# Two transformer blocks on one core: five expert loads put among the second block's weight loads, three raw buffers there, and each expert's six halves loaded in a row

## The reference, cut to what matters

```python
g_prob = softmax(xt @ w_rg + b_rg); g_w, g_idx = top_k(g_prob, 1)
e_top, e_loc = top_k(e_logits_of_that_group, 2)
e_w = softmax(e_top) * g_w
...
def run_block(args):
    xb, e = args
    return (silu(xb @ w_gate[e]) * (xb @ w_up[e])) @ w_down[e]
...
x = x + gate2 * ffn
return rms_norm(x, g_final)
```

## Time and profile before

| | |
|---|---|
| median of 3 runs | 1094.51 us |
| the profiled execution, its own time | 1095.95 us |
| its span, first to last instruction | 1094.2 us |
| mean granted TensorE clock | 0.98 |
| PE busy | 1022.7 us (93%) |
| DVE, ACT busy | 493.4 us (45%), 389.9 us (36%) |
| read from HBM over the span | 325.88 MB, 299 GB/s |

### The profile page before, as it was taken

One profiled execution on the slowest core, in us unless ns is written; L12 is line 12 of the kernel. 1 busy time (PEld: TensorE's weight loads), 2 busy tenths in 40 slices (PEclk: granted clock), 3 DMA queues, 4 the chain that ended last, 5 costly groups with the idle time before them and its releaser, 6 DMA issues.

```text
span 1094.2 us, 13601 instructions
## 1 busy us (share of the span) xinstructions
PE 1022.7 (93%) x5616; PEld 700.9 (64%) x5616; DVE 493.4 (45%) x683; ACT 389.9 (36%) x575; POOL 22.3 (2%) x42
## 2 busy tenths in 40 slices
PE   5999999999999999798999699999999999999883
PEld 4888878888999888697787444444444444443331
DVE  4477667987967745765645511111111111101003
ACT  5644544446435443664734221111111111111112
POOL 0000000010000000100000000000000000000000
PEclk9999999999999999898999799999999999999997
DMA  9977448976887655354444699999999999999991
GB/s 332 338 256 258 160 164 294 315 268 224 287 300 260 235 198 187 104 179 127 181 154 162 265 405 421 421 421 421 422 420 421 421 420 422 421 420 421 422 394 45
DMA packets 86305, 327.87 MB, mean 300 GB/s; under 512 B 5744, under 2 KB 5776, under 8 KB 61536
## 3 DMA queue, kind: packets, MB, share of 16 engines
q1 hardware_dynamic: 84896, 323.45, 77.0%
q0 software_dynamic: 1344, 3.50, 1.0%
HBM read 325.88 MB, written 1.05 MB: 299 GB/s over the span
## 4 chain that ended last, share of the span: by engine, by line
PE 40%; DMA 13%; DVE 3%; ACT 2%; issue 1%; DVEq 0%; ACTq 0%
PE bank L899 15%; DMA e_wlo<-in_w_expert_up 8%; PE bank L922 7%; PE bank L868 3%; DMA es<-in_w_expert_up 3%; DMA raw<-in_w_expert_up 2%; PE bank L937 2%; PE bank L539 2%; PE bank L540 2%; PE bank L543 1%; PE bank L908 1%; PE bank L511 1%; PE bank L515 1%; PE bank L514 1%; PE bank L883 1%
## 5 line engine op out<-in xcount | busy, mean ns | idle before, releaser
L1441 DVE TENSOR_TENSOR wlo<-raw,whi 128x2048 fp32r<-128x2048 f32 x90 | 205.9, 2290 | 105.8 <-ACT whi L985 105.2
L985 ACT ACTIVATE whi<-raw 128x2048 fp32r<-128x2048 f32 x90 | 171.6, 1912 | 98.3 <-PE bank L515 37.9
L2032 DVE SCALAR_TENSOR_TENSOR YL<-bank,wsl,YH 128x512 fp32r<-128x512 f32 x32 | 24.0, 751 | 269.1 <-ACT YH L1369 269.1
L899 PE MATMUL bank<-raw,XT 128*64 128x512 f32 x400 | 90.8, 596 | 5.2 <-DMA raw<-in_w_expert_up 5.2
L899 PE MATMUL bank<-e_whi,XT 128*64 128x512 f32 x192 | 88.5, 604 | 6.7 <-DMA e_wlo<-in_w_expert_up 6.7
L514 PE MATMUL bank<-wlo,hh 128*128 128x512 f32 x224 | 88.5, 395 | 2.9 <-DVE wlo L1441 2.9
L511 PE MATMUL bank<-whi,hh 128*128 128x512 f32 x224 | 89.2, 398 | 1.0 <-ACT whi L985 1.0
L899 PE MATMUL bank<-e_wlo,XT 128*64 128x512 f32 x192 | 88.6, 605 | 0.0
L515 PE MATMUL bank<-whi,hl 128*128 128x512 f32 x224 | 88.3, 394 | 0.0
L539 PE MATMUL bank<-fh,whi 128*128 128x256 f32 x256 | 73.6, 287 | 1.2 <-DVE fl L1611 1.2
L1430 DVE SCALAR_TENSOR_TENSOR ada_acc<-raw,silu_c,ada_acc 128x512 f32<-128x512 f32 x96 | 72.0, 750 | 2.5
(11 more groups left out here) (359 smaller groups left out, 1902.5 us busy)
## 6 DMA issues: line engine op xcount, KB each, us to landing
raw<-in_w_in SPq DMA_DIRECT2D x42, 1024.0 KB, 5.4
raw<-in_w_ff SPq DMA_DIRECT2D x32, 1024.0 KB, 5.4
raw<-in_w_expert_gate SPq DMA_DIRECT2D x25, 1024.0 KB, 22.3
raw<-in_w_expert_up SPq DMA_DIRECT2D x25, 1024.0 KB, 23.0
raw<-in_w_ada SPq DMA_DIRECT2D x24, 1024.0 KB, 5.9
e_whi<-in_w_expert_gate SPq DMA_DIRECT2D x24, 1024.0 KB, 24.2
e_wlo<-in_w_expert_up SPq DMA_DIRECT2D x24, 1024.0 KB, 25.2
raw<-in_w_expert_down SPq DMA_DIRECT2D x22, 1024.0 KB, 25.2
```

Source lines behind the costliest of these rows:

```text
L899: m = e.matmul(b[64 * w:64 * w + 64, :], K.XT[j // 4 % 2][:, k, j % 4, :], K.weights(halves[w])[:, 512 * c:512 * c + 512], start=k == 0, s ...
L985: e.activation(whi[n % RING][:, :], raw[h.raw][:, :], ACT.Copy).then_inc(S["hi"], 1)
L1441: e.tensor_tensor(wlo[n % RING][:, :], raw[h.raw][:, :], whi[n % RING][:, :].bitcast(F32), ALU.subtract).then_inc(S["lo"], 1)
```

## The change

It has four parts. (1) Halves 96 to 113 use only the first three raw buffers (`i % (RAW // 2)` from `LATE` on), and a half waits for the one that was last in its buffer, kept as `before`. (2) The list of the experts' sixteen buffers becomes `es12`, raw3, raw4, raw5, `es7`, raw0, raw1, raw2, then as before; SP issues loads 0 to 4 after halves 98, 99, 100, 101 and 112. (3) The loads' order becomes expert by expert: gate, up, gate, up, down, down, so that expert j's are loads 6j to 6j + 5. (4) PE's order of use stays. `used_up` holds for every expert half its place in that order, and replaces the load's own number where a semaphore's value is wanted.

```diff
+LATE = 96
...
-        self.raw = i % RAW
-        self.loaded = 16 * (i // RAW + 1)
+        self.raw, self.before = raw, before
+        self.loaded = before.loaded + 16 if before else 16
...
+            raw = i % RAW if i < LATE else i % (RAW // 2)
+            half = Half(i, kind, src, chunks, info, len(self.of[kind]), raw, self.in_raw.get(raw))
+            self.in_raw[raw] = half
...
+        self.used_up, n_used = {}, 0
         for base, n, one in ((0, NE, fixed), (NE, NOV, moving)):
+            for j in range(n):
+                for w, hf in ((0, 0), (1, 0), (0, 1), (1, 1), (2, 0), (2, 1)):
+                    one(j, w, hf)
             for j in range(n + 1):
-                for hf in range(2 if j < n else 0):
-                    one(j, 0, hf)
-                    one(j, 1, hf)
+                for w, hf in ((0, 0), (1, 0), (0, 1), (1, 1)) * (j < n):
+                    n_used += 1
+                    self.used_up[base + j, w, hf] = n_used
                 for hf in range(2 if j > 0 else 0):
-                    one(j - 1, 2, hf)
+                    n_used += 1
+                    self.used_up[base + j - 1, 2, hf] = n_used
...
         buffer(slot("es12", 12, [128, 2048]), "es12", 0)
-        buffer(slot("es7", 7, [128, 2048]), "es7", 0, "mix_mm", MIX["m"] + 4)
-        for h in self.halves[-RAW:]:
-            buffer(self.raw[h.raw], f"raw{h.raw}", h.loaded, "lo", h.nth + 1)
+        for r in (*range(RAW // 2, RAW), None, *range(RAW // 2)):
+            if r is None:
+                buffer(slot("es7", 7, [128, 2048]), "es7", 0, "mix_mm", MIX["m"] + 4)
+            else:
+                h = self.in_raw[r]
+                buffer(self.raw[r], f"raw{r}", h.loaded, "lo", h.nth + 1)
...
-        if h.i >= RAW:
-            o = K.halves[h.i - RAW]
+        o = h.before
+        if o:
...
         if i >= n:
-            e.wait_ge(S["eused"], i - n + 1)
+            e.wait_ge(S["eused"], K.used_up[K.experts[i - n][1:]])
...
+    early = {LATE + 2 + k: k for k in range(4)}
+    early[len(K.halves) - 2] = 4
     for h in K.halves:
         load(h)
-    for i in range(K.n_static):
+        if h.i in early:
+            load_expert(early[h.i], K.experts[early[h.i]][0])
+    for i in range(len(early), K.n_static):
```

More of the change, by code:

```diff
@@ L60, with __init__ @@
 class Half:
-    def __init__(self, i, kind, src, chunks, info, nth):
+    def __init__(self, i, kind, src, chunks, info, nth, raw, before):
         self.i, self.kind, self.src, self.chunks, self.info = i, kind, src, chunks, info
         self.nth = nth
-        self.raw = i % RAW
-        self.loaded = 16 * (i // RAW + 1)
+        self.raw, self.before = raw, before
+        self.loaded = before.loaded + 16 if before else 16
 class Sems(dict):
@@ L219, in order_weights @@
         A, self.halves, self.of, n_ada = self.A, [], {"mm": [], "ada": []}, [0]
-        self.half_of = {}
+        self.half_of, self.in_raw = {}, {}
         def add(kind, src, chunks, info=None):
-            self.of[kind].append(Half(len(self.halves), kind, src, chunks, info, len(self.of[kind])))
-            self.halves.append(self.of[kind][-1])
+            i = len(self.halves)
+            raw = i % RAW if i < LATE else i % (RAW // 2)
+            half = Half(i, kind, src, chunks, info, len(self.of[kind]), raw, self.in_raw.get(raw))
+            self.in_raw[raw] = half
+            self.of[kind].append(half)
+            self.halves.append(half)
         def cols(w, r0, c0):
@@ L271, in expert @@
             self.half_of[j, w, hf] = len(self.experts)
-            self.experts.append((src, j))
+            self.experts.append((src, j, w, hf))
         def fixed(e, w, hf):
@@ L1351, in gate_up @@
         def gate_up(j):
-            e.wait_ge(S["eused"], K.half_of[j, 1, 1] + 1)
+            e.wait_ge(S["eused"], K.used_up[j, 1, 1])
             if j > 1:
@@ L1364, in down @@
         def down(j):
-            e.wait_ge(S["eused"], K.half_of[j, 2, 1] + 1)
+            e.wait_ge(S["eused"], K.used_up[j, 2, 1])
             e.wait_ge(S["pt"], 2 * j + 2)
@@ L1375, in gathered @@
             if p > 1 and q == 1:
-                e.wait_ge(S["eused"], K.half_of[4 * p - 5, 1, 1] + 1)
+                e.wait_ge(S["eused"], K.used_up[4 * p - 5, 1, 1])
             for c in range(2):
@@ L2024, in middle @@
             if j > 1:
-                e.wait_ge(S["eused"], K.half_of[j - 2, 2, 1] + 1)
+                e.wait_ge(S["eused"], K.used_up[j - 2, 2, 1])
             e.tensor_tensor(K.HT[j % 2][:, :, :], K.SG[j % 2][:, :, :],
```

## The result

The changed kernel takes 1104.92 us (median of 4, 1104.69 to 1105.91) against 1094.52 us (the kernel before has a fourth run here): 10.4 us more. The ratio on record is 1.0103, 95% interval 1.0089 to 1.0117; it isn't the plain quotient of the two medians (1.0095), and makes 11.3 us (9.7 to 12.8). Forecast were 1105.5 us and a range of 1101.0 to 1109.5.

The account below looks back on a forecast made before the run. The DMA load stream was taken to bound the stage's end. Early loads 0, raw buffers 0, two places in the order +5.0 and load 20 held +6.0 made +11.0 on 1094.5: 1105.5 us, range 1101 to 1109.5.

Parts of the forecast that it names:

- What sets the end: Expert stage: the DMA stream from load 16, started by PE leaving its first buffer, and the last expert's first need.
- Early loads, three raw buffers: Second block's halves: five earlier expert loads gain 0, since buffers are full anyway; three raw buffers cost 0.
- The rival in which the early loads come off the stream: Pause of 616 to 624: if not full buffers, early loads save 12.4 us, 1087.1 in all; chance (faster) 0.04.
- (a): Load order at expert 31: its first up half is load 187 instead of 185, two loads later, +5.0 us.
- (b): SP's queue at load 20: held until expert 0's first down half is used, DMA pauses, +6.0 us; bounds 4.5 and 6.3.
- PE's lead: PE ahead of the load stream: used up at expert 11 or 12, near 770 to 780 us, instead of near 905.
- The tail: After the last wait for an up load, at expert 31: fixed work of 39.1 us, unchanged.
- Smaller lag: Rival on load landings: they lag 2 to 4 us less after the pause, giving 1100 to 1103; chance 0.13.
- SP held again and again: Rival on SP's queue: it runs dry before down halves in 28 experts, 28 us, 1133; chance 0.10 with late loads.
- The restart latency: Load 20's restart: 0.9 us from issue to first packets; the page's 0.6 would make the sum 10.7, not 11.0.
- Issuing early: Skill's advice to issue a DMA early and wait late; the prediction held the expert loads were early enough already.
- The upper end: Top of the range: +5.0, +6.3, 1 more, and one late load of 3 us, given as 1109.5.

Follow-up runs that it names:

- e5: Kernel before with only expert 30's two down halves loaded ahead of expert 31's gate and up halves; +5.9 us (4.4 to 7.4).
- e8: Kernel before plus sixteen matmuls of constants on PE, eleven ahead of the first gathering and five before expert 31's first matmul; -1.3 us (-2.4 to -0.3).
- e2: Changed kernel's early loads and three raw buffers, with the experts' halves in the old order; -0.2 us (-1.4 to 1.0) against the kernel before.
- e3: Kernel before with down halves loaded ahead of the next expert's gate and up only for experts 16 to 30; +5.6 us (4.1 to 7.0).
- e9: Kernel before plus only the eleven matmuls of constants on PE ahead of the first gathering; -1.9 us (-3.0 to -0.8).
- e4: Kernel before with down halves loaded ahead only for experts 0 to 7, then the old order; +4.6 us (3.2 to 6.1).
- e7: Kernel before with twelve expert buffers instead of sixteen and the new order of halves, no early loads; +21.4 us (19.7 to 23.1).
- e6: Kernel before with twelve expert buffers instead of sixteen, old order; +9.5 us (7.9 to 11.2).
- e10: Kernel before plus only the five matmuls of constants on PE before expert 31's first matmul; -0.4 us (-1.5 to 0.5).

## Why the prediction was right

- *What sets the end.* Right. The stream from load 16 on, whose start PE sets, and the place of the last first need. e5 moved the place by two loads and cost 5.9 us. e8's profile moved the start by 3.3 us and the last need came at 1049.93 instead of 1055.12; over all its runs the gain is small. The kernel before first waits for a load at 919.3, not near 905 as the prediction put it.
- *Early loads, three raw buffers: 0.* Right by e2 (-0.2 us). The rival in which the early loads come off the stream is out: no load went out between 602.3 and 623.4. Half 113, queued behind load 4, went out at 550.40 and was split at 585.32. Half 100 went out at 458.99 (459.54 was forecast), and ACT's splits that had 467.28 and 478.75 before came at 466.92 and 478.39.
- *(a), two places, +5.0.* The times of e3 and e5 say 5.6 and 5.9 with intervals that hold 5.0; their profiles' intervals are 4.4 and 4.3 over the 434.0 that before, e2, e8 and e9 average (435.1, 433.9, 433.2, 433.6).
- *(b), load 20 held, +6.0.* Issued at 639.73 and 641.45 where 639.96 and 641.67 were read off the old trace. e4: 4.6 us (3.2 to 6.1) in time, 6.2 in its interval. A count of the bytes agrees: from 616 to 700 the engines moved 370 GB/s before and 338 after, 2.7 MB less, which is 6.4 us of the stream; e2's 369 and e4's 340 make 5.8 us (the streams with the hole began 0.2 and 0.5 us earlier, which comes on top). The time alone can't tell 6.0 from the lower bound, 4.5.
- *PE's lead.* Put at expert 11 or 12, near 775; it was expert 13, at 794.7. The landing there lagged by 4.7 us (794.74 against 640.6 + 60 x 2.49 = 790.0), not 5.6, and 0.9 us of lag shifts the meeting by nearly one expert, since the two paces differ by 1.16 us only. That also puts the waits at 22.2 instead of about 25. At the end it made little: the last need came at 1064.91, where 1066 was said.
- *The tail, 39.1 us.* It was 1102.8 - 1064.9 = 37.9. Before, PE ran expert 31's first half in 5.11 us, at 1.2 GHz after a wait of 2.99 us; after, in 3.65 us, after a wait of 1.99. The prediction carried the fallen clock over. In e2, after 2.10 us, the clock fell too (5.35), and the like 39.3 us followed: it differs between executions, and why is not shown. The profile of before had also an odd interval, 16.5 us from expert 30's first need to expert 31's, where e2 has 15.0. Both errors pull the profiled span (1102.8, for 1105.2 forecast) and not the medians, which differ by 10.4 where 11.0 was forecast.
- *Smaller lag.* This rival came true by about 1 us of its 3: load 187's landing lagged by 6.0 us (1064.91 against 640.6 + 168 x 2.49 = 1058.9), load 185's in the kernel before by 7. The interval grew by 10.0 us over the profile before, or by 11.1 over the 434.0; as one execution moves it by 1 us, an agreement closer than that is luck.
- *SP held again and again.* Not seen: share 1.01 from 700 to 1050, and 1.01 in e7 with four buffers fewer. Load 27 went out at 656.14, where 656.3 was forecast; the 0.3 us lost at 658 come behind it.
- *The restart latency.* In both traces the first packets come some 0.9 us after the issue begins. Counted from the issue's end, 0.33 us later, the gap is 0.5 to 0.8 us before and 0.4 to 0.7 after. The Trainium skill, "DMA: Bandwidth & Descriptors", section Specifications, gives about 0.6 us, which lies in that, so the prediction's 10.7 follows only if the page's figure is counted from the issue's beginning; the times can't tell 10.7 from 11.0.
- *Issuing early.* e2's early loads gain nothing (-0.2 us), since every buffer is full before its reader comes. The Trainium skill, same page, section Rules for kernel authors, advises to issue a DMA early and wait for it late; in this case there was nothing left to gain by it.
- *The upper end.* The prediction's own terms give 1094.5 + 12.3 + 3 = 1109.8, not 1109.5; nothing hangs on it.

## What to carry to other kernels

Where a stream of loads runs through a ring of buffers and ends the kernel, count what lies in the buffers when the reader leaves the first one: filling them earlier is worth nothing once they are full, a further buffer is worth one load, and an earlier reader moves the stream with it. Load in the order of use. A half loaded ahead of its use can cost twice, once because what is needed first now lands later, and once because its buffer is free later and everything behind it in the issuing queue stands. The second cost comes only where the queue runs dry meanwhile, which here was once, before load 20. The price of the first is set at the last reader alone, so one swapped pair near the end costs what fifteen did.

## What the runs showed of the hardware

- Landings lag behind the bytes once many loads are queued: 1.8 us for load 19, 4.6 for load 27, 5.6 for load 131 and 7 for load 185 in the kernel before, with 421 GB/s moved. In the changed kernel it was 4.7 at load 79 and 6.0 at load 187. So it grew by 2.3 us at most over the last 160 loads.
- An issue of a 1 MB load on SP's queue took 0.33 to 0.43 us while 16 to 19 us passed from issue to landing (700 to 740, kernel before), and mostly 2.13 us where 26 to 29 us passed (900 to 940), which is some 11 loads at 2.49 us. The stream stayed full, at 421 GB/s.
- The gathering's 32 matmuls took from 3.99 (e8, at 2.4 GHz throughout) to 6.66 us (e6) in the profiled executions, by when the granted clock rises from 1.2 to 2.4 GHz in them. They also began at 612.8 to 614.9. The two together moved expert 0's start between 616.8 and 621.5, and with it the start of the load stream.
- A wait of 2 us for a load left the clock up in some executions (after: 1.99 us, then 3.65 us for 16 matmuls) and down in others (e2: 2.10 us, then 5.35). The length of the wait doesn't decide it: after 1.98 us the 16 matmuls took 3.65 us in e2 (at 1039.14) and 5.35 in e10 (at 1038.44).
